# Two transformer blocks in fp32: gate and up products with high and low activations in one 512-column stretch, chunk products in halves

## The chip, the cores and the metric

The kernel runs on one core of a Trainium2 chip. The metric is the device time of one execution in microseconds; lower is better. A core has a matrix engine (TensorE, PE in the rows; its weight loads are PEld), a vector engine (VectorE, DVE), a scalar engine (ScalarE, ACT), GpSimd (POOL) and SyncE (SP), which here issues nearly all the weight transfers. Each engine works through its own list of instructions in order and waits on semaphores for the others. PE writes only to PSUM; ACT and DVE read it from there.

## What is computed

The reference is two blocks of layers, each of depth 2, on 256 tokens of width 1024, all in fp32. The change touches the first block alone:

```python
def first_block(x, p, positions, ...):
    h = x
    for i in range(DEPTH):                      # DEPTH = 2
        a = rms_norm(h, attn_norm[i])
        proj = a @ w_in[i]                      # split into the inputs of three mixers
        y_da  = diff_attention(...)
        y_ssd = ssd_mixer(...)                  # chunked scan, chunks of 128
        y_gla = gla_mixer(...)                  # gated linear attention, chunks of 64
        h = h + concat(y_da, y_ssd, y_gla) @ w_out[i]
        f = rms_norm(h, ffn_norm[i])
        h = h + (silu(f @ w_ffn_gate[i]) * (f @ w_ffn_up[i])) @ w_ffn_down[i]   # D_FF = 2816
        h = h + sigmoid(h @ ple_w_gate[i]) * (p[i] @ ple_w_proj[i])
    return h
```

In `ssd_mixer` the product within a chunk is `y_diag = einsum('bclsgr,bcsgrp->bclgrp', cb * decay, xdt)`: for each of 2 chunks and 8 heads a 128 x 128 map, lower triangular, times 128 x 64 values. The second block (a gated scan and a latent attention, modulated by `silu(c) @ ada_w + ada_b`) needs the modulation rows `c @ ada_w`; the kernel computes those in the layers of the first block, in three turns of PSUM called mod0, mod1 and mod2 in each layer.

## The kernel before

**Precision.** Large products are made from pairs. Weights and activations are split into a high part, rounded to float32r, and a low part, what is left. ACT writes the high part of a piece of weights (`split_high`, one ACTIVATE at L563), DVE subtracts and writes the low part (`split_low`, L570). A product is then a `triple` of matmuls: weights high by activations low, weights low by activations high, and high by high, all three added up in one stretch of PSUM. Small products (transposes, chunk products, modulation) are plain fp32 matmuls. In the profile a plain fp32 matmul shows as two records, a transpose as one. L2575 is the line of `mm`, L2578 that of `tr`.

**Weights.** They stream through a ring of four slots of 1 MB in a fixed order. SP issues the transfer of a piece when PE has ended the piece four places ahead of it (L2176, and L2208 for `ada_w`); ACT splits it, DVE splits it, PE uses it.

**PSUM in turns.** The half named `pg` is two buffers of 1024 columns, `pm` two more. `GEMM = Turns(pg, ...)` holds a list of turns by name; turn number k lies in buffer k modulo 2 and may begin when turn k - 2 is released by whoever read it. `M = Turns(pm, ...)` is the same for the small products. So the position of a name in these lists decides whom PE waits for.

**Around the chunk products.** In each layer, after the input projections and the scores of attention, PE runs in program order: state, pv and gla_att (`pm`), six transposes kendT (`pm`), modulation(1), the states gla_st0 (`pm`, from kendT as ACT copied it), the 16 chunk products ydiag into one turn of `pg`, the eight transposes mix0, gla_st1, modulation(2), yoff, and then the output projection `wo_products`. ACT meanwhile copies: pv with its squares (L2479, L2482), kendT (L2488), then `gates_silu` (a table load and a Silu over 2048 columns, L2420), `modulation_rows(1)` (L2350, which releases the turn mod1), the split of wo1, the copy of ydiag (L2479), and so on. DVE folds gla_st0 into running states (`gla_state`, L3237 and L3240; the second call releases gla_st0), splits wo1, makes the low part of mix0 (L3255), folds gla_st1, adds ydiag and yoff (L3276 to L3280) and norms the SSD output (up to L3249). PE waits for that norm before the transposes mix1. The list of `pg` turns there is z, mod0, gg, mod1, ydiag, mod2, wo_t0, wo_t1. The list of `pm` turns is gla_att, kendT, gla_st0, mix0, gla_st1, yoff: gla_st1 takes the buffer of gla_st0.

**Gate and up.** D_FF has 22 blocks of 128 columns. A piece `gu{j}_{k}` holds one block of gate weights and the same block of up weights. `columns_by_tokens` takes two pieces a turn: for each piece, for gate and up, for the 8 chunks of the contraction, a triple with 128 x 128 weights stationary and 256 tokens moving. Two pieces fill one turn of 1024 columns. ACT then takes Silu of the gate half (L2519), DVE multiplies by the up half (L3320), rounds (L3322), subtracts (L3324) and releases the turn. The down projection (`rows_to_width`) follows.

## Time and profile before

| | |
|---|---|
| median of 3 runs | 1776.08 us |
| lowest, highest | 1774.67, 1778.15 us |
| the profiled execution | 1776.09 us |
| its span, first to last instruction | 1774.0 us |
| mean granted TensorE clock | 0.996 of full speed |
| PE busy, weight loads busy | 96%, 84% of the span |
| DVE, ACT, POOL busy | 68%, 51%, 3% |
| gate and up products of layer 0, of layer 1 | from 219.28 to 344.26 us, from 640.82 to 765.8 us |
| output stage of the mixers of layer 0, of layer 1 | 146 to 182 us, 566 to 604 us |

The profile is one execution seen by the hardware profiler. Times in its rows are us from the first instruction. An instruction's own duration contains its pipeline, so matmuls in a stream overlap: what one costs is the distance from its start to the next start, and a run of n matmuls that lasts T with a last duration of d costs (T - d) / (n - 1) each. "idle before <-" says how long the engine stood still before a row and who released it.

### The profile page before, as it was taken

How to read it: one execution, taken by the hardware profiler on the slowest of the kernel's cores; microseconds unless marked ns; L12 is line 12 of the kernel's file. 1: busy time of each engine (PE TensorE's matmuls, PEld its weight loads, DVE VectorE, ACT ScalarE, POOL GpSimd, SP SyncE). 2: the span in 40 equal slices, each digit the busy share in tenths (PEclk: the TensorE clock that was granted, in tenths of full speed). 3: DMA queues.
4: the chain of work that ended last, by engine and by line, in shares of the span. 5: the costliest groups of instructions: out<-in, count | busy, mean ns of one | idle time of the engine just before them, and what ended most of it. 6: DMA issues, size and time to landing. Idle time of an engine off the chain costs nothing.

```text
span 1774.0 us, 34217 instructions
## 1 busy us (share of the span) xinstructions
PE 1709.9 (96%) x14302; PEld 1487.3 (84%) x14302; DVE 1207.2 (68%) x1673; ACT 902.5 (51%) x1112; POOL 44.5 (3%) x47
## 2 busy tenths in 40 slices
PE   6999999998999999999999999999999989999998
PEld 5877799987987789988988888888888867899896
DVE  5888755546678765545557768678677795577874
ACT  5564443335475443334554556455454553466772
POOL 2000000000000000000000000000000000000130
PEclk9999999998999999999999999999999999999999
DMA  8557568654457566655321322222212122352112
GB/s 202 186 190 298 154 169 200 190 190 149 145 169 265 208 166 191 190 190 166 99 88 61 93 72 73 77 68 85 73 61 85 60 96 96 113 176 62 48 63 104
DMA packets 255241, 238.20 MB, mean 134 GB/s; under 512 B 32800, under 2 KB 218192, under 8 KB 254832
## 3 DMA queue, kind: packets, MB, share of 16 engines
q1 hardware_dynamic: 253952, 233.21, 42.4%
q0 software_dynamic: 1136, 2.81, 0.6%
q8 instruction: 113, 1.85, 0.4%
q14 instruction: 40, 0.33, 0.1%
HBM read 234.94 MB, written 1.05 MB: 133 GB/s over the span
## 4 chain that ended last, share of the span: by engine, by line
PE 81%; DVE 7%; ACT 4%; DMA 3%; SPq 2%; DVEq 2%; issue 1%; ACTq 1%
PE pg L2575 34%; PE pg L1279 34%; PE pm L1279 7%; PE pm L2575 2%; PE pm L1282 2%; SPq L2198 2%; DMA ring<-in_ada_w 1%; DVE ring_r L570 1%; DMA ring<-in_hg_w_in 1%; PE pm L2578 1%; DVE ring_r L1734 1%; ACT ring_r L563 1%; DVEq L1770 1%; DVE ring L1768 1%; DMA ring<-in_w_in 0%
## 5 line engine op out<-in xcount | busy, mean ns | idle before, releaser
L570 DVE TENSOR_TENSOR ring_r<-ring,ring_r 128x2048 fp32r<-128x2048 f32 (+1 forms) x126 | 283.5, 2260 | 151.2 <-ACT ring_r L563 145.6
L2575 PE MATMUL pg<-ring_r,work_r 128*128 128x512 f32 (+1 forms) x1776 | 377.3, 372 | 5.5 <-DVEq L3047 2.9
L2575 PEld LDWEIGHTS pg<-ring_r,work_r 128*128 128x128 f32 x1776 | 306.1, 189 | 68.6 <-issue 8.4
L1279 PE MATMUL pg<-ring_r,work_r 128*128 128x512 f32 (+3 forms) x1280 | 355.6, 383 | 5.1 <-DVE work_r L1740 3.5
L2575 PE MATMUL pg<-work_r,ring_r 128*128 128x256 f32 x2688 | 318.7, 281 | 6.8 <-DVE ring_r L570 3.7
L2575 PEld LDWEIGHTS pg<-work_r,ring_r 128*128 128x128 f32 x2688 | 317.3, 188 | 8.2 <-DVE ring_r L570 4.5
L563 ACT ACTIVATE ring_r<-ring 128x2048 fp32r<-128x2048 f32 (+1 forms) x126 | 237.1, 1890 | 167.6 <-DMA ring<-in_w_ffn_up 67.7
L1279 PE MATMUL pg<-ring_r 128*128 128x512 f32 (+3 forms) x752 | 284.2, 378 | 2.5 <-DVEq L783 1.4
L1279 PEld LDWEIGHTS pg<-ring_r,work_r 128*128 128x128 f32 x1280 | 235.5, 188 | 50.6 <-DVEq L1735 4.2
L1279 PE MATMUL pg<-work_r,ring_r 128*128 128x512 f32 (+1 forms) x976 | 264.1, 360 | 0.0
L1279 PEld LDWEIGHTS pg<-work_r,ring_r 128*128 128x128 f32 x976 | 173.0, 189 | 26.9
L1279 PEld LDWEIGHTS pg<-ring_r 128*128 128x128 f32 x752 | 141.6, 188 | 26.5 <-DVEq L783 1.6
L775 ACT ACTIVATE ring_r<-ring 128x1024 fp32r<-128x1024 f32 x80 | 84.9, 1061 | 53.9 <-DMA ring<-in_hg_w_in 46.9
L782 DVE TENSOR_TENSOR ring_r<-ring,ring_r 128x1024 fp32r<-128x1024 f32 x80 | 98.0, 1225 | 17.0 <-ACTq L776 10.9
L1768 DVE TENSOR_TENSOR work<-work 128x1024 f32<-128x1024 f32 x56 | 66.1, 1222 | 23.3 <-PE pm L1279 21.9
L1768 DVE TENSOR_TENSOR ring<-ring,work 128x1024 f32<-128x1024 f32 x56 | 66.1, 1222 | 15.7 <-PE pm L1279 14.3
L1279 PE MATMUL pg<-work_r,work_r 128*128 128x256 f32 (+1 forms) x360 | 73.7, 322 | 0.6 <-DVEq L1735 0.6
L968 ACT COPY prm<-ring 128x1024 f32<-128x1024 f32 x28 | 31.9, 1138 | 72.1 <-DVEq L1770 44.6
L968 ACT COPY prm<-work 128x1024 f32<-128x1024 f32 x28 | 32.0, 1144 | 65.4 <-DVEq L1770 42.1
L1279 PEld LDWEIGHTS pg<-work_r,work_r 128*128 128x128 f32 x360 | 57.6, 190 | 5.9 <-DVEq L1735 0.9
L1279 PE MATMUL pm<-work 128*32 128x32 f32 (+1 forms) x928 | 59.5, 233 | 0.0
L1279 PEld LDWEIGHTS pm<-work 128*32 128x32 f32 (+1 forms) x928 | 56.3, 146 | 2.8 <-issue 0.8
(382 smaller groups left out, 1858.6 us busy)
## 6 DMA issues: line engine op xcount, KB each, us to landing
ring<-in_w_in SPq DMA_DIRECT2D x36, 1024.0 KB, 5.1
ring<-in_ada_w SPq DMA_DIRECT2D x24, 1024.0 KB, 7.1
ring<-in_hg_w_in SPq DMA_DIRECT2D x48, 512.0 KB, 3.7
ring<-in_w_ffn_gate SPq DMA_DIRECT2D x44, 512.0 KB, 3.9
ring<-in_w_ffn_up SPq DMA_DIRECT2D x44, 512.0 KB, 5.2
ring<-in_w_ffn_down SPq DMA_DIRECT2D x22, 1024.0 KB, 4.8
ring<-in_hg_w_in SPq DMA_DIRECT2D x64, 256.0 KB, 2.9
ring<-in_w_out SPq DMA_DIRECT2D x12, 1024.0 KB, 4.9
```

What stands on the lines that cost most here:

```text
L563: W.high_done(A.activation(hi, W.raw(i, name)[:, 0:hi.shape[1]], ACT.Copy))
L570: W.low_done(V.tensor_tensor(lo, W.raw(i, name)[:, 0:lo.shape[1]], W.hi(i, name).bitcast(f32), ALU.subtract))
L775: A.activation(HS.hi(name), HW.slot(name), ACT.Copy)
L782: V.tensor_tensor(HS.lo(name), HW.slot(name), HS.hi(name).bitcast(f32), ALU.subtract)
L968: A.copy(k_level.rearrange("p (n r m) -> p n r m", r=2, m=1 << lev), halves_of(b, KF, KB, lev))
L1279: return T.matmul(out_, lhsT, rhs, start=first, stop=last)
L1282: return T.transpose(out_, in_, ident)
L1734: V.tensor_tensor(MP.lo(name)[:, 0:n], MP.raw(name)[:, 0:n], MP.hi(name)[:, 0:n].bitcast(f32), ALU.subtract)
L1768: V.tensor_tensor(ap[:, :, :, r, :], ap[:, :, :, r, :], dec[:, :, :, 1 - r, 0].unsqueeze(3).to_broadcast([P, 2, 512 // m, m]), ALU.mult)
L1770: event.set(dve.drain())
L2198: sp.dma_start(dst, src).then_inc(loaded_prm, 16)
L2575: return T.matmul(out_, lhsT, rhs, start=first, stop=last)
```

## The change

1. **Gate and up.** A view `work_pairs` of the whole work tile in float32r lets one matmul read the high and the low activations of a chunk as two stretches of 256 columns, one behind the other (`later_pair`). With the high weights stationary it writes 512 columns: high by high in the first 256, high by low in the last 256. A second matmul of 256 columns adds low weights by high activations to the first half. So 2 matmuls stand in place of a triple's 3, with the same number of moved columns. Each of the 22 pieces is a turn of PSUM of its own (gate in one bank, up in the other).
2. **Behind it.** ACT copies the high-by-low halves out of PSUM, DVE adds the other halves and releases the turn, ACT takes Silu of the gate, and DVE multiplies, rounds and subtracts, now on 256 columns a piece; the latter three run one piece later.
3. **Chunk products.** ydiag becomes two turns, ydiag0 and ydiag1, one a chunk. Each 128 x 64 product becomes two with 64 weight columns each, whose results go to partitions 0 to 63 and 64 to 127.
4. **Order on PE.** modulation(1) moves ahead of the kendT transposes, and ydiag0 and ydiag1 move ahead of gla_st0.
5. Two events for qT and kT become one that counts to two. Nothing moves by it.

The core of the diff:

```diff
         GEMM = Turns(pg, sem("gemm_filled"), [sem("gemm_free0"), sem("gemm_free1")],
-                     ["daq", "dak", "xbc0", "xbc1", "gqk", "dav", "gv", "z", "mod0", "gg", "mod1", "ydiag", "mod2", "wo_t0", "wo_t1"]
-                     + [f"gu{j}" for j in range(FC // 2)] + ["dn_t0", "dn_t1"] + ple_pieces)
+                     ["daq", "dak", "xbc0", "xbc1", "gqk", "dav", "gv", "z", "mod0", "gg", "mod1", "ydiag0", "ydiag1", "mod2", "wo_t0", "wo_t1"]
+                     + gu_pieces + ["dn_t0", "dn_t1"] + ple_pieces)
...
+        def later_pair(c):
+            row = work_pairs[:]
+            return bass.AP(row.tensor, row.offset + start(aT) + c * S, [list(row.ap[0]), [start(low_f) - start(aT), 2], [1, S]])
...
                 gates_silu()
                 modulation_rows(1)
                 split_high(act, i, wo_pieces[1])
-                part_in("ydiag", xdt, None, GEMM)
+                for t in range(NT):
+                    GEMM.wait_filled(act, f"ydiag{t}", i)
+                    GEMM.release(A.copy(xdt[:, t * 512:(t + 1) * 512], GEMM.buf(f"ydiag{t}")[:, 0:512]), f"ydiag{t}")
+                e_part.set(act.drain())
...
+                def gate_up_part(j):
+                    name = gu_pieces[j]
+                    GEMM.wait_filled(act, name, i)
+                    if j > 1:
+                        e_gu.wait(act, i, j - 1)
+                    src = GEMM.buf(name).rearrange("p (f r n) -> p f r n", f=2, r=2)
+                    e_gate.set(A.copy(q3(gate_up[:, (j % 2) * 512:(j % 2) * 512 + 512], 2), src[:, :, 1, :]))
+
+                def gate_silu(j):
+                    gate = gate_up[:, (j % 2) * 512:(j % 2) * 512 + S]
+                    e_gsum.wait(act, i, j + 1)
+                    e_gate.set(A.activation(gate, gate, ACT.Silu))
+
                 for k in range(3, len(later_pieces)):
-                    j = (k - 3) // 2
-                    if k % 2 == 0 and j < FC // 2:
-                        GEMM.wait_filled(act, f"gu{j}", i)
-                        e_sgate.set(A.activation(sgate[:, (j % 2) * 512:(j % 2) * 512 + 512], GEMM.buf(f"gu{j}")[:, 0:512], ACT.Silu))
+                    j = k - 3
+                    if j < FC:
+                        gate_up_part(j)
+                    if 0 < j <= FC:
+                        gate_silu(j - 1)
...
+                def gate_and_up(name):
+                    wh, wl = weights(name, KC, 256)
+                    GEMM.wait_free(pe, name, i)
+                    order = [(f, c) for f in range(2) for c in range(KC)]
+                    if name == gu_pieces[0]:
+                        order = [(f, 2 * q + c) for q in range(4) for f in range(2) for c in range(2)]
+                    for f, c in order:
+                        if name == gu_pieces[0] and f == 0 and c % 2 == 0:
+                            e_aT.wait(pe, i, 4 + c // 2 + 1)
+                        both, cs = GEMM.buf(name)[:, f * 512:(f + 1) * 512], slice(f * P, (f + 1) * P)
+                        if c == 0:
+                            mm(both, wh[:, c, cs], later_pair(c), True, False)
+                            mm(both[:, 0:S], wl[:, c, cs], A_LATER[0][:, c, :], False, False)
+                        else:
+                            mm(both[:, 0:S], wl[:, c, cs], A_LATER[0][:, c, :], False, False)
+                            last = mm(both, wh[:, c, cs], later_pair(c), False, c == KC - 1)
+                    GEMM.done(last)
...
                 M.done(last)
+                modulation(1)
                 M.wait_free(pe, "kendT", i)
...
-                modulation(1)
...
+                e_mt.wait(pe, i)
+                for t in range(NT):
+                    GEMM.wait_free(pe, f"ydiag{t}", i)
+                    for hd in range(SSD_H):
+                        for q in (0, 64):
+                            at = t * 1024 + hd * P + q
+                            last = mm(GEMM.buf(f"ydiag{t}")[q:q + 64, hd * 64:(hd + 1) * 64], big[:, at:at + 64],
+                                          xdt[:, t * 512 + hd * 64:t * 512 + (hd + 1) * 64])
+                    GEMM.done(last)
                 e_kendT.wait(pe, i)
                 e_gv.wait(pe, i)
                 gla_states("gla_st0", (0, 1))
...
+                def gate_up_sum(j):
+                    name, both = gu_pieces[j], q3(gate_up[:, (j % 2) * 512:(j % 2) * 512 + 512], 2)
+                    e_gate.wait(dve, i, at_part(j))
+                    src = GEMM.buf(name).rearrange("p (f r n) -> p f r n", f=2, r=2)
+                    GEMM.release(V.tensor_tensor(both, both, src[:, :, 0, :], ALU.add), name)
+                    e_gsum.set(dve.drain())
```

On PE, at the chunk products of layer 0, the rows of before are these. The transposes in the first row are kendT, `ring,prm` is modulation(1), the first 128x256 is gla_st0, 128x64 is ydiag:

```order
L2578 MATMUL pm<-cst,work 128x128 [waits mixer_psum_free1]
L2578 MATMUL pm<-cst,work 128x128 x5
L2575 MATMUL pg<-ring,prm 32x256 [waits ada_weights_ready0,gemm_free0]
...
L2575 MATMUL pg<-ring,prm 32x256 x7
L2575 MATMUL pm<-work 128x256 [waits mixer_psum_free0,gv_in,kendT_in]
L2575 MATMUL pm<-work 128x256 x3
L2575 MATMUL pg<-work 128x64 [waits gemm_free1,ssd_maps]
L2575 MATMUL pg<-work 128x64 x15
L2578 MATMUL pm<-cst,work 128x128 [waits mixer_psum_free1,mixer_out]
```

The same place on PE after the change (64x64 are the halves of ydiag0 and ydiag1):

```order
L2602 MATMUL pg<-ring,prm 32x256 [waits ada_weights_ready0,gemm_free0]
...
L2602 MATMUL pg<-ring,prm 32x256 x7
L2605 MATMUL pm<-cst,work 128x128 [waits mixer_psum_free1]
L2605 MATMUL pm<-cst,work 128x128 x5
L2602 MATMUL pg<-work 64x64 [waits gemm_free1,ssd_maps]
L2602 MATMUL pg<-work 64x64 x15
L2602 MATMUL pg<-work 64x64 [waits gemm_free0]
L2602 MATMUL pg<-work 64x64 x15
L2602 MATMUL pm<-work 128x256 [waits mixer_psum_free0,gv_in,kendT_in]
L2602 MATMUL pm<-work 128x256 x3
L2605 MATMUL pm<-cst,work 128x128 [waits mixer_psum_free1,mixer_out]
```

modulation(1) now stands first, the chunk products stand ahead of gla_st0, and their second half has a wait of its own, on gemm_free0: the buffer that mod1 was in.

On ACT at the same place, after the change (L2497 copies kendT, L2429 is `gates_silu`, L2359 is `modulation_rows(1)`, L571 splits wo1, L2504 copies ydiag0 and ydiag1); before it the rows stood in this same order, with one copy of 1024 columns for ydiag:

```order
L2497 COPY work<-pm 128x768 [waits mixer_psum_filled]
L2429 ACT_TABLE_LOAD
L2429 ACTIVATE work<-work 128x2048
L2359 COPY work<-pg 128x256 [waits gemm_filled]
L571 ACTIVATE ring_r<-ring 128x2048 [waits gemm_filled,weights_ready2]
L2504 COPY work<-pg 128x512 [waits gemm_filled] x2
L2482 ACTIVATE work_r_12800<-pm,prm 128x1024 [waits mixer_psum_filled]
```

Only the copy of ydiag changed here: no row moved past another.

On PE in the middle of a gate or up block, before (work_r_22040 is the low part of the activations, work_r_4096 the high part):

```order
L2575 MATMUL pg<-work_r_4096,ring_r 128x256 x2
L2575 MATMUL pg<-work_r_22040,ring_r 128x256
L2575 MATMUL pg<-work_r_4096,ring_r 128x256 x2
L2575 MATMUL pg<-work_r_22040,ring_r 128x256
```

and after:

```order
L2602 MATMUL pg<-work_pairs,ring_r 128x256
L2602 MATMUL pg<-work_pairs,ring_r 128x512
L2602 MATMUL pg<-work_pairs,ring_r 128x256
L2602 MATMUL pg<-work_pairs,ring_r 128x512
```

Three matmuls of 256 columns became one of 256 and one of 512.

## Rows read from the trace of the kernel before

**Rows 1.** The page: the chain that ended last, share of the span by engine.

```profile
PE 81%; DVE 7%; ACT 4%; DMA 3%; SPq 2%; DVEq 2%; issue 1%; ACTq 1%
```

**Rows 2.** Timeline, PE, gate and up products of layer 0: start, duration, line, operation, count.

```profile
225.44 0.73 PE L2575 MATMUL pg<-work_r,ring_r 128*128 128x256 f32 x4 [0.28 <-DVE ring_r L570]
...
230.72 112.52 PE L2575 MATMUL pg<-work_r,ring_r 128*128 128x256 f32 x954
```

**Rows 3.** Timeline, PE: streams of 512-column matmuls, and a change from 256 to 512.

```profile
24.50 16.77 PE L2575 MATMUL pg<-ring_r,work_r 128*128 128x512 f32 x71 [0.23 <-DVE ring_r L570]
...
349.77 50.48 PE L2575 MATMUL pg<-ring_r,work_r 128*128 128x512 f32 x222
...
882.06 0.28 PE L1279 MATMUL pg<-work_r,ring_r 128*128 128x256 f32 x1
...
882.54 0.40 PE L1279 MATMUL pg<-ring_r 128*128 128x512 f32 x1
...
883.93 0.39 PE L1279 MATMUL pg<-ring_r 128*128 128x512 f32 x1
```

**Rows 4.** Groups by line and form, DVE and ACT, from 225.4 to 344.2 us.

```profile
L570 DVE TENSOR_TENSOR ring_r<-ring,ring_r 128x2048 fp32r<-128x2048 f32 x22 | 50.3, 2292 | 28.0 <-ACT ring_r L563 26.6
L563 ACT ACTIVATE ring_r<-ring 128x2048 fp32r<-128x2048 f32 x21 | 40.2, 1913 | 33.3 <-DMA ring<-in_w_ffn_up 30.6 <-DMA ring<-in_w_ffn_down 2.7
L3320 DVE TENSOR_TENSOR work<-work,pg 128x512 f32<-128x512 f32 x10 | 6.9, 688 | 18.9 <-ACT work L2519 18.9
L2519 ACT ACTIVATE work<-pg 128x512 f32<-128x512 f32 x10 | 6.0, 597 | 36.6 <-PE pg L2575 36.6
```

**Rows 5.** Timeline, PE, around the chunk products of layer 0.

```profile
145.90 5.13 PE L2575 MATMUL pm<-work 128*128 128x256 f32 x44 [0.37 <-ACT work L2462]
152.17 0.88 PE L2578 MATMUL pm<-cst,work 128*128 128x128 f32 x6 [1.13 <-ACT work L2482]
152.97 3.66 PE L2575 MATMUL pg<-ring,prm 128*32 128x256 f32 x64
156.56 1.99 PE L2575 MATMUL pm<-work 128*128 128x256 f32 x8
158.39 3.68 PE L2575 MATMUL pg<-work 128*128 128x64 f32 x32
161.91 1.04 PE L2578 MATMUL pm<-cst,work 128*128 128x128 f32 x8
162.79 1.03 PE L2575 MATMUL pm<-work 128*128 128x256 f32 x4
...
166.73 1.07 PE L2575 MATMUL pg<-ring,prm 128*32 128x256 f32 x16 [0.18 <-DMA ring<-in_ada_w]
...
168.51 3.79 PE L2575 MATMUL pg<-ring_r,work_r 128*128 128x512 f32 x15
```

**Rows 6.** Timeline, ACT, the same place.

```profile
153.08 0.80 ACT L2488 COPY work<-pm 128x768 f32<-128x768 f32 x1 [0.96 <-PE pm L2578]
...
157.27 0.37 ACT L2350 COPY work<-pg 128x256 f32<-128x256 f32 x1
```

**Rows 7.** Timeline, DVE, the same place: the two folds of gla_st0.

```profile
158.66 1.20 DVE L3237 COPY work<-pm 64x128 f32<-64x128 f32 x4
159.94 1.43 DVE L3240 SCALAR_TENSOR_TENSOR work<-work,pm 64x128 f32<-64x128 f32 x4
```

**Rows 8.** Timeline, PE: layer 1, the same place, and the next wait of layer 0.

```profile
179.01 1.09 PE L2578 MATMUL pm<-cst,work 128*128 128x128 f32 x8 [0.21 <-DVEq L3250]
...
588.24 1.07 PE L2575 MATMUL pg<-ring,prm 128*32 128x256 f32 x16 [1.61 <-DMA ring<-in_ada_w]
```

**Rows 9.** Timeline, SP, the issues of the `ada_w` pieces of modulation(2).

```profile
154.10 2.96 SPq L2208 DMA_DIRECT2D ring<-in_ada_w  x4
```

**Rows 10.** Stretches of the trace, PE alone: length, busy (x), granted clock, DMA share, GB/s.

```profile
441.00:443.00 2.00, 2.00 (x5) 0.50 0.00 0
```

**Rows 11.** Timeline, PE: the long wait between the layers.

```profile
436.28 3.68 PE L2578 MATMUL pm<-cst,work 128*128 128x128 f32 x16 [4.96 <-DVE work L3012]
```

## What the change should do to the time

> **What bounds the kernel now.** I read the chain that ended last first: 81% of the span is PE [rows 1], and PE is busy for 96% of it. So an instruction taken from PE's stream is worth its distance to the next start, and a new wait of PE is worth its length, unless something later waits anyway. Then I read PE's timeline in the two places that the change touches. In the gate and up products PE runs without a wait: after one of 0.28 us for the low weights of the second piece, 954 matmuls stand in one row [rows 2]. Around the chunk products PE's list is short pieces of work that alternate with copies on ACT and DVE, with waits of 1.13 us for ACT (L2482) and of 0.18 us for `ada_w` [rows 5]. The second of these is 1.61 us in layer 1 [rows 8]. There ACT and DVE must be read beside PE [rows 6, 7].
>
> **Gate and up: what a group of matmuls costs.** Before, 954 matmuls of 256 columns take 112.52 us, the last lasting 0.28: (112.52 - 0.28) / 953 = 0.1178 us each, 0.3533 a triple. After, a triple is one of 512 columns and one of 256. Moved columns are the same, so the gain can only be the fixed cost of one matmul. The trace has long streams of 512 at two rates [rows 3]: (50.48 - 0.39) / 221 = 0.2267, and (16.77 - 0.39) / 70 = 0.2340, which holds a small hesitation. It has no alternation of the two sizes. Right behind 256-column matmuls the 512s come every (883.93 - 882.54) / 6 = 0.2317 us (the shown rows are the first and the last of seven starts), and the 256s ahead of them every (882.54 - 882.06) / 4 = 0.120. In the new stream every 512 follows a 256, which is this case, and every 256 follows a 512.
>
> A low estimate of the pair is 0.2267 + 0.1178 = 0.3445, and one from the rows around the change of size is 0.2317 + 0.120 = 0.3517. I take the middle, 0.348. As ends I keep 0.2267 + 0.110 = 0.337 (0.110 is (161.91 - 158.39) / 32, the pace of matmuls with 128 weight columns and hardly any moved ones, [rows 5]) and 0.2340 + 0.120 = 0.354, which is no gain at all. That the moving operand is now in two stretches lies inside these ends; no row shows it, and the order of reads by rows of 256 is what the triples did.
>
> A piece has 16 triples, a layer 22 pieces. The first piece gains nothing: it is fed by DVE, and the second starts when DVE has split its weights, at 225.44, whatever PE did [rows 2]. So 21 x 16 = 336 groups a layer: 336 x (0.3533 - 0.348) = 1.8 us, **3.6 us in both layers**, with ends of 11 us and -0.5 us.
>
> The Trainium skill, page "TensorE: Matmul & The Clock Gate", section "Back-to-back issue gap", gives a warm gap of the columns over 2.4 GHz plus 2.5 ns. By it a triple would cost 327.5 ns and the new pair 325.0, an estimate of 0.8 us a layer and 1.7 in all in place of 3.6. The rows above show about 11 ns over the columns for a 256 and 13 to 18 for a 512, so the trace doesn't agree with its constant, and I go by the rows.
>
> **Gate and up: what moves to ACT and DVE.** A piece lasts 16 x 0.348 = 5.6 us on PE. In it ACT has a split (1.91 us), a copy of 512 columns out of PSUM (as L2519, 0.60) and a Silu of 256 (about 0.35, somewhat over half of 0.60): 2.9 us. DVE has a split (2.29), a sum of 512 (as L3320, 0.69) and three steps of 256 (the product at 512, L3320, takes 0.69; I take 1.1 for the three halves): 4.1 us [rows 4]. Both fit. The turn is released after a copy and a sum, about 1.4 us after PE filled it, and PE wants the buffer 5.6 us after: cost zero, and if ACT or DVE were held up PE would have 4 us before it noticed. Weights: piece k is split after piece k - 3 is done and used two pieces later, at least 11 us for about 5 us of splitting. Transfers are issued by PE's progress as before. Cost zero.
>
> **Chunk products and their order: PE step by step, layer 0.** The 1.13 us wait goes, since modulation(1) needs nothing that is late: its 64 records at 152.97 show no wait for `ada_w` [rows 5]; that they are there 2 us earlier is not shown, and I take it so, since the transfers were issued one behind the other as modulation(0) freed their slots, well before. It starts at 145.90 + 5.13 = 151.03 and takes 156.56 - 152.97 = 3.59: to 154.62. The kendT transposes take 0.80: to 155.42. Then ydiag0. A 64-weight product can't be paced by 0.110 any more; its 64 moved columns cost 64 x 0.229 / 256 = 0.057 (gla_st0: (158.39 - 156.56) / 8 = 0.229 for 256), and two halves write different partitions. The modulation matmuls, four strips of 32, take 3.59 / 64 = 0.056 each where a lone one of 256 columns takes 0.229: strips run side by side. So 64 records x 0.057 / 2 = 1.8 us in both turns (0.9 each) where 3.52 stood; side by side or not is open, and the end without it is 3.65. ydiag0 ends at 156.3.
>
> Now ydiag1 waits for the buffer of mod1, and what releases it is ACT's L2350. ACT's order has not changed: copy of kendT, table load and Silu of 2048 columns, then L2350. From the start of the kendT copy to the end of L2350 is 157.27 + 0.37 - 153.08 = 4.56 us [rows 6]. Before, kendT came early and mod1 ran beside the Silu. Now kendT is there at 155.5, so L2350 ends at 160.1. **PE waits 3.8 us** and does ydiag1 until 161.0. Behind the waiting matmul are gla_st0, mix0, gla_st1 and modulation(2). gla_st0 (1.83) ends at 162.9. DVE, which was at work on it from 158.66 to 161.37 [rows 7], starts at 163.0 and releases it after 2.71 us, at 165.7. PE does mix0 (0.88, to 163.7) and **waits 2.0 us** for that release before gla_st1. From gla_st1 to the output products took 168.51 - 162.79 = 5.72 us with 0.18 of waiting, so 5.54: they start at 171.3, **2.8 us late**.
>
> The wait for `ada_w` in modulation(2) goes: its four pieces are issued as modulation(1) frees their slots, from 154.10 before [rows 9], 1.9 us earlier now, and PE comes 3 us later. That is the 0.18 above, and in layer 1 it is 1.61. Layer 1 has the same schedule 420.08 us later ((588.24 - 1.61) - (166.73 - 0.18), the moments at which PE began to wait), so it loses 2.8 - (1.61 - 0.18) = 1.4 us. Is the loss taken back later? The next wait is for the norm of the SSD output, 0.21 us at 179.01 [rows 8]; its input is the copy of yoff, which is late by the same 2.8, so nothing is there to take it. **Sum: +4.2 us.** The ends are +3 (shorter transitions) and +6 (halves not side by side: 0.9 us more a layer before DVE can start).
>
> **The sum.** +4.2 - 3.6 = +0.6 us. The profiled execution took 1776.09 us, the median of three is 1776.08, so the forecast is 1776.7 us. A measurement of this kernel can tell about 0.2%, or 3.6 us, from no change. The forecast is inside.
>
> **Rivals.**
>
> *The pairs run faster.* If weight loads are all that holds a 256 behind a 512, the group costs under 0.342 and the gain is over 7.6 us. At 0.340 it is 672 x 0.0133 = 8.9, and the time is 1776.1 + 4.2 - 8.9 = 1771.4. For it: one matmul in three is gone and the fixed cost is some 11 ns. Against it: 512s behind 256s are slower in the rows, 0.2317. Chance 0.17.
>
> *PE doesn't wait at ydiag1.* If L2350 came in time, ydiag would end at 157.3, gla_st0 at 159.1, DVE at 161.8, and the output products would start some 1.2 us early in layer 0 and 2.6 in layer 1: 1776.1 - 3.8 - 3.6 = 1768.7. The order and the durations on ACT speak against it. Chance 0.06.
>
> *The clock falls in the new wait.* After a wait of 4.96 us [rows 11] PE is granted 0.50, its 1.2 GHz level, and still has it from 441 to 443 us [rows 10]; what it did before was to stand idle. The new wait of 3.8 us is shorter, but longer than the 1.61 us before the last part of modulation(2) in layer 1; over the whole span the mean grant is 0.996, so the short waits cost no clock. If the clock falls, ydiag1 and gla_st0 (2.7 us) take twice as long, and gla_st1 likewise: 3.5 us a layer. In both layers: 1776.7 + 7 = 1783.7; in one, 1780.2. It is decided by whether the idle time of 3.8 us is enough. Chance 0.14.
>
> *Slow pairs and chunk halves that run one after the other.* Pairs at 0.354 (+0.5) and 0.9 us a layer: 1776.1 + 4.2 + 0.5 + 1.8 = 1782.6. Chance 0.06.
>
> **How the numbers follow.** The forecast has 0.57, all of it within 0.2%. Faster is the first two rivals, 0.23; slower the last two, 0.20; same 0.57. The range reaches to the first rival below, 1771, and above to the clock falling in one layer with some of the open cost, 1781.5; that leaves out about 0.2.
>
> **What would show it.** The group: the count and length of PE's stream in the gate and up products, 0.348 x 16 = 5.57 us a piece where it was 5.65; 704 matmuls a layer for 1056. The wait: a row of 64-column weights with some 3.8 us idle before it, ended by ACT's copy of mod1, and one of 2 us before gla_st1, ended by DVE; the wait for `ada_w` gone in both layers; the output products 2.8 us later after the start of pv in layer 0. The clock: 1.00 in these stretches. I am wrong if ydiag1 starts without a wait, if the group costs less than 0.342 or more than 0.354, or if PE waits anywhere inside the gate and up products.

## The result, and the profile after

The changed kernel takes 1781.94 us (median of 20 executions, 1777.91 to 1784.1) beside 1776.38 for the kernel before on the same chip (20 executions, 1774.49 to 1779.57). The ratio is 1.0027, with a 95% interval of 1.0021 to 1.0033: **slower by 4.8 us**, and by 5.6 in the medians. The forecast was 1776.7 and no change, with a range from 1771 to 1781.5. The profiled execution took 1783.84 us, with a span of 1781.7 and a mean granted clock of 0.992.

Timeline of PE, around the chunk products of layer 0, to be read beside [rows 5]:

```profile
147.36 5.13 PE L2602 MATMUL pm<-work 128*128 128x256 f32 x44 [0.38 <-ACT work L2471]
152.42 3.66 PE L2602 MATMUL pg<-ring,prm 128*32 128x256 f32 x64
156.01 0.87 PE L2605 MATMUL pm<-cst,work 128*128 128x128 f32 x6
156.81 1.15 PE L2602 MATMUL pg<-work 128*64 128x64 f32 x32
161.54 1.98 PE L2602 MATMUL pg<-work 128*64 128x64 f32 x32 [3.57 <-ACT work L2359]
163.45 3.78 PE L2602 MATMUL pm<-work 128*128 128x256 f32 x8
167.02 1.23 PE L2605 MATMUL pm<-cst,work 128*128 128x128 f32 x8
170.10 1.41 PE L2602 MATMUL pm<-work 128*128 128x256 f32 x4 [1.85 <-DVE work L3281]
171.44 5.01 PE L2602 MATMUL pg<-ring,prm 128*32 128x256 f32 x64
176.38 1.13 PE L2602 MATMUL pm<-work 128*128 128x256 f32 x4
177.16 1.05 PE L2602 MATMUL pg<-ring_r,work_r 128*128 128x512 f32 x3
```

The order is the one foreseen: the 1.13 us ahead of the kendT transposes is gone, PE stands 3.57 us before ydiag1 until ACT has copied mod1 (L2359), and then stands 1.85 us before gla_st1 for DVE, and modulation(2) is one row without a wait for `ada_w`. But two durations don't fit. The second turn of 32 half products lasts 1.98 us where the first lasts 1.15, and gla_st0 lasts 3.78 us for 8 matmuls that took 1.99 before [rows 5]. modulation(2) lasts 5.01 where modulation(1), the same 64 matmuls, lasts 3.66. The stretches of the same trace tell why (length, then PE, PEld, DVE, ACT, POOL busy, granted clock, DMA share, GB/s):

```profile
158.00:160.00 2.00, 0.00 (x0) 0.00 (x0) 1.85 (x2) 1.99 (x2) 0.00 (x0) 1.00 1.01 418
160.00:162.00 2.00, 0.46 (x8) 0.46 (x10) 0.00 (x0) 1.74 (x3) 0.00 (x0) 0.64 1.02 420
162.00:164.00 2.00, 2.00 (x31) 1.83 (x28) 0.00 (x0) 2.00 (x3) 0.00 (x0) 0.50 1.03 418
164.00:166.00 2.00, 2.00 (x6) 1.60 (x5) 0.00 (x0) 0.52 (x2) 0.00 (x0) 0.50 0.74 295
166.00:168.00 2.00, 2.00 (x11) 1.62 (x10) 0.64 (x3) 0.00 (x0) 0.00 (x0) 0.65 0.01 2
168.00:170.00 2.00, 0.25 (x3) 0.01 (x1) 1.86 (x6) 1.11 (x1) 0.00 (x0) 1.00 0.00 0
170.00:172.00 2.00, 1.90 (x12) 1.01 (x16) 1.91 (x2) 0.00 (x0) 0.00 (x0) 0.70 0.04 8
172.00:174.00 2.00, 2.00 (x24) 0.86 (x20) 1.83 (x3) 0.00 (x0) 0.00 (x0) 0.50 0.00 0
```

PE does nothing from 158 to 160, and before its wait is over the granted clock begins to fall (0.64 from 160 to 162) to 0.50, the 1.2 GHz level. It falls a second time behind the wait of 1.85 us. In the kernel before it is 1.00 in every such stretch here, in both layers. In layer 1 of after it falls twice as well: gla_st0 lasts 3.55 us and modulation(2) 4.97. There the 32 half products right behind the wait still last 1.15 us, at the full clock, and the fall comes only with gla_st0 behind them.

The Trainium skill, page "TensorE: Matmul & The Clock Gate", Part 1, section "What's actually happening", says of this clock that "the default state is throttled, and activity releases the throttle". The trace agrees as far as it goes: the clock falls in a wait or shortly behind one, and is back at 1.00 from 168 us on, when PE has worked through gla_st0, until the next wait.

From the start of pv (147.36) to the first output product (177.16) is 29.80 us in layer 0 and 28.75 in layer 1. Before it was 22.61 (168.51 - 145.90, [rows 5]) and 24.04. That is +7.2 and +4.7, where the forecast had +2.8 and +1.4. Behind it nothing is caught up and nothing more is lost in layer 0: from the first output product to the first gate and up product is 50.77 us in both kernels.

The two profiled executions also differ where nothing was changed, so the medians are a better measure than these two. After comes to pv in layer 0 1.46 us later (147.36 against 145.90), and to pv in layer 1 5.73 us later, where 1.46 + 7.2 - 1.1 = 7.6 would be due: between the layers, behind the wait of [rows 11], its clock was at 0.50 for a shorter time. And it has one more fall, behind a wait of 1.89 us in the input projections of layer 0 (a row of PE's timeline, then a stretch as above):

```profile
70.40 13.38 PE L2602 MATMUL pg<-work_r,ring_r 128*128 128x256 f32 x96 [1.89 <-DVE ring_r L578]
...
72.00:74.00 2.00, 2.00 (x11) 2.00 (x11) 1.92 (x5) 0.94 (x2) 0.00 (x0) 0.50 0.37 140
```

This one cost nothing: from the start of that row to the next is 13.22 us here, and 13.20 in another execution of the same program (e10 below), where the clock stays at 1.00 and PE waits 1.53 us for DVE halfway instead.

Timeline of PE, gate and up products of layer 0, beside [rows 2]:

```profile
227.93 5.80 PE L2602 MATMUL pg<-work_pairs,ring_r 128*128 128x512 f32 x32 [1.54 <-DVEq L3078]
234.10 117.84 PE L2602 MATMUL pg<-work_pairs,ring_r 128*128 128x512 f32 x672 [0.37 <-DVE ring_r L578]
351.78 8.59 PE L2602 MATMUL pg<-ring_r,work_r 128*128 128x512 f32 x37
```

21 pieces of 16 pairs take 351.78 - 234.10 = 117.68 us, so a pair is 0.3502 by this row, where a triple was 0.3533: by its instructions, a matmul behind a 256 starts after 117.0 ns, one behind a 512 after 233 (229 to 239). The stage is 123.85 us long (before: 124.98), so it is 1.13 us a layer shorter, 2.3 in all, where the forecast had 3.6. The pairs make 336 x 3.1 ns = 1.04 of the 1.13; the other 0.1 is not placed.

ACT and DVE behind it, groups by line and form in that stretch (count, then busy us, mean ns, idle before), beside [rows 4]:

```profile
L3358 DVE TENSOR_TENSOR work<-work,pg 128x512 f32<-128x512 f32 x21 | 14.5, 689 | 20.3 <-ACT work L2534 20.3
L2534 ACT COPY work<-pg 128x512 f32<-128x512 f32 x21 | 12.3, 587 | 57.3 <-PE pg L2602 57.3
L3369 DVE TENSOR_TENSOR work_r<-work,work_r 128x256 fp32r<-128x256 f32 x20 | 8.5, 426 | 1.6
L3365 DVE TENSOR_TENSOR work<-work 128x256 f32<-128x256 f32 x20 | 8.5, 425 | 2.7
L2539 ACT ACTIVATE work<-work 128x256 f32<-128x256 f32 x20 | 8.4, 421 | 0.0
L3367 DVE CAST work_r<-work 128x256 fp32r<-128x256 f32 x20 | 5.9, 293 | 1.6
```

DVE's four steps of a piece sum to 0.689 + 0.425 + 0.293 + 0.426 = 1.83 us, ACT's two to 1.01; with the splits that is 4.1 and 2.9 of 5.6 us, as forecast, and PE waits nowhere inside but the 0.37 us at the second piece (0.28 before).

### The profile page after: what moved, and what is told of

Same layout as the page of the kernel before. It is cut to its first block, busy times and chain, and to the rows that moved or that the text cites. A ratio compares the mean times of both kernels' runs of the same rounds, so it can differ in the third digit from the quotient of the medians.

```text
span 1781.7 us, 33287 instructions
## 1 busy us (share of the span) xinstructions
PE 1712.6 (96%) x13662; PEld 1455.1 (82%) x13662; DVE 1246.3 (70%) x1783; ACT 926.4 (52%) x1180; POOL 44.4 (2%) x47
## 4 chain that ended last, share of the span: by engine, by line
PE 81%; DVE 7%; ACT 4%; SPq 2%; DVEq 2%; DMA 1%; issue 1%; ACTq 1%
PE pg L1288 34%; PE pg L2602 34%; PE pm L1288 8%; PE pm L2602 3%; PE pm L1291 2%; SPq L2207 2%; DVE ring_r L578 1%; PE pm L2605 1%; DMA ring<-in_w_in 1%; ACT ring_r L571 1%; DVEq L1779 1%; DVE ring L1777 1%; DVE ring_r L1743 1%; DMA ring<-in_hg_w_in 0%; SPq L2185 0%
## 5 line engine op out<-in xcount | busy, mean ns | idle before, releaser
L571 ACT ACTIVATE ring_r<-ring 128x2048 fp32r<-128x2048 f32 (+1 forms) x126 | 237.2, 1888 | 108.3 <-DMA ring<-in_w_ffn_down 53.3
L2602 PE MATMUL pg<-work_pairs,ring_r 128*128 128x512 f32 (+1 forms) x1408 | 247.3, 337 | 3.8 <-DVEq L3078 3.1
L2602 PEld LDWEIGHTS pg<-work_pairs,ring_r 128*128 128x128 f32 x1408 | 215.1, 188 | 35.9 <-issue 3.5
L1288 PEld LDWEIGHTS pg<-work_r,ring_r 128*128 128x128 f32 x976 | 173.0, 189 | 27.3
L2534 ACT COPY work<-pg 128x512 f32<-128x512 f32 x44 | 25.8, 587 | 122.1 <-PE pg L2602 122.1
L2602 PE MATMUL pg<-work_r,ring_r 128*128 128x256 f32 x576 | 71.0, 285 | 2.3 <-DVE ring_r L578 2.3
L2602 PEld LDWEIGHTS pg<-work_r,ring_r 128*128 128x128 f32 x576 | 70.0, 192 | 3.3 <-DVE ring_r L578 3.1
```

The lines of the kernel that those rows point to most:

```text
L571: W.high_done(A.activation(hi, W.raw(i, name)[:, 0:hi.shape[1]], ACT.Copy))
L1288: return T.matmul(out_, lhsT, rhs, start=first, stop=last)
L2534: e_gate.set(A.copy(q3(gate_up[:, (j % 2) * 512:(j % 2) * 512 + 512], 2), src[:, :, 1, :]))
L2602: return T.matmul(out_, lhsT, rhs, start=first, stop=last)
```

## The experiments

All times are medians; "ratio" is to the kernel before on the same chip, with its 95% interval. The last column is the time from the start of pv to the first output product in layers 0 and 1 of the profiled execution, with * where the granted clock fell in it. The kernels did not all run on one chip: the kernel before took 1777.35 us beside e1 to e4, 1776.23 beside e5 to e8 and 1776.86 beside e9 to e12. So a difference of medians between two of these groups is good to about 1 us, and the ratios are given beside it.

| kernel | us | ratio | pv to output products |
|---|---|---|---|
| before | 1776.38 | | 22.61, 24.04 |
| after | 1781.94 | 1.0027 [1.0021, 1.0033] | 29.80*, 28.75* |
| e1_fill | 1779.82 | 1.0013 [1.0005, 1.0022] | 27.19*, 25.56 |
| e2_rows_first | 1771.6 | 0.9966 [0.9954, 0.9978] | 23.40*, 22.03 |
| e3_mod_back | 1774.35 | 0.9982 [0.9973, 0.999] | 23.18, 24.87* |
| e4_gu_only | 1775.83 | 0.9984 [0.9976, 0.9993] | 22.57, 23.90 |
| e5_best | 1769.56 | 0.996 [0.9945, 0.9975] | 21.18, 21.69 |
| e6_triples | 1772.83 | 0.9983 [0.9974, 0.9993] | 23.40*, 21.96 |
| e7_grouped | 1770.26 | 0.9966 [0.9954, 0.9977] | 23.40*, 22.09 |
| e8_full | 1774.45 | 0.999 [0.9981, 0.9998] | 23.13, 24.76* |
| e9_two_fills | 1779.29 | 1.0011 [1.0002, 1.002] | 25.57, 25.56 |
| e10_after_again | 1782.06 | 1.0025 [1.0014, 1.0037] | 27.11*, 25.55 |
| e11_rows_again | 1771.48 | 0.9961 [0.9949, 0.9974] | 23.46*, 21.96 |
| e12_best_again | 1770.59 | 0.9964 [0.9951, 0.9978] | 20.84, 21.95 |

The theory was: the new wait before ydiag1 costs its length, and the granted clock that falls in it or behind it costs the rest. The rival: the two orders and the pairs have costs of their own that the profile shows only in part, and the clock is chance.

**e1_fill: the wait filled with idle products.** The edit against after; the products go to the half of ydiag0's buffer that nobody reads:

```diff
                 for t in range(NT):
+                    if t:
+                        for _ in range(4):
+                            mm(GEMM.buf("ydiag0")[:, 512:1024], ones, cst[:, 0:512])
                     GEMM.wait_free(pe, f"ydiag{t}", i)
```

> The changed kernel with four fp32 matmuls of constants, 512 columns each, put on PE between ydiag0 and ydiag1 (into the unused bank of ydiag0's buffer, read by nobody). They last about 3.5 us, as long as the wait for the buffer of mod1, and lengthen nothing. Theory: the wait lets the granted clock fall to 0.50, which costs 4.4 us in layer 0 and 3.3 us in layer 1 of the profiled run beside the waits themselves. Then with the engine kept at work the clock stays at 1.00, ydiag1 to gla_st0 take 2.7 us, and the time is about 1776.4 + 4.2 - 2.2 = 1778.4 us. Rival: the slow ydiag1, gla_st0 and modulation(2) come from something else (the half-width form, the order): then the time stays at 1782 us and the stretch stays slow.

Measured: 1779.82. In its profile gla_st0 lasts 1.99 us again, in both layers. In layer 0 the clock still falls, behind the other wait:

```profile
162.29 1.15 PE L2602 MATMUL pg<-work 128*64 128x64 f32 x32
163.37 1.99 PE L2602 MATMUL pm<-work 128*128 128x256 f32 x8
165.21 1.04 PE L2605 MATMUL pm<-cst,work 128*128 128x128 f32 x8
168.24 1.46 PE L2602 MATMUL pm<-work 128*128 128x256 f32 x4 [2.00 <-DVE work L3284]
169.63 4.96 PE L2602 MATMUL pg<-ring,prm 128*32 128x256 f32 x64
```

So the first fall is gone in both layers and the second is not in layer 0. The median is 1.4 us over the expectation, which had not thought of that second place; the fall there cost 27.19 - 25.56 = 1.6 us in this profile.

**e9_two_fills and e10_after_again: both waits filled, and the changed kernel beside it.** Two such products more, ahead of gla_st1:

```diff
                 mixed_transposes(0)
+                for _ in range(2):
+                    mm(GEMM.buf("ydiag1")[:, 512:1024], ones, cst[:, 0:512])
                 gla_states("gla_st1", (2,))
```

> The changed kernel with four idle products of 512 columns of ones between the two turns of chunk products (as e1_fill) and two more ahead of the second GLA state products, where TensorE otherwise waits 2.00 us for VectorE. No operation of another engine moves. Theory (the granted clock falls in waits): the modulation products behind that wait take 3.66 us in both layers and no stretch of that part shows less than 1.00; e1_fill had 4.96 us in its first layer and 1.00 in its second. 1778.6 us, some 1.2 us under e1_fill's 1779.82, and 3.3 us under the changed kernel. Rival (the clock falls for the traffic of the chip or at random, whatever TensorE does there): as e1_fill, 1779.8 us, and falls in the profile as before.

> The changed kernel itself beside e9_two_fills, on the same chip. All theories: 1782 us, and a wait of 3.57 us ahead of the second turn of chunk products in both layers, with a granted clock under 1.00 behind it both times.

Measured: 1779.29 against 1782.06 on the same chip, 2.8 us less in the medians with six products more a layer. The intervals of these two ratios overlap, 1.0002 to 1.002 and 1.0014 to 1.0037; that of after's 20 executions, 1.0021 to 1.0033, and e9's do not. e9 shows 1.00 in every stretch of this part in both layers, and its two layers take the same time, 25.57 and 25.56. By its ratio, though, it isn't told from e1 (1.0011 and 1.0013), so what the second fill is worth alone stays open. Nor do the two profiled executions show the gain: e9's took 1779.91 us, 1.5 more than e10's, mostly because the fall between the layers lasted longer in it (last section). The gain stands on the medians.

e10 is the same program as after and tells more. Its profiled execution took 1778.38, 5.5 us less than that of after. The waits are nearly the same (2.00 us before gla_st1 where it was 1.85 and 1.87), but in this part the clock fell once where it fell four times. Timeline of PE, e10, layer 0 and then layer 1:

```profile
157.60 1.15 PE L2602 MATMUL pg<-work 128*64 128x64 f32 x32
162.33 1.97 PE L2602 MATMUL pg<-work 128*64 128x64 f32 x32 [3.57 <-ACT work L2359]
164.23 2.72 PE L2602 MATMUL pm<-work 128*128 128x256 f32 x8
...
583.92 1.15 PE L2602 MATMUL pg<-work 128*64 128x64 f32 x32 [3.58 <-ACT work L2359]
585.00 1.99 PE L2602 MATMUL pm<-work 128*128 128x256 f32 x8
```

And its stretches:

```profile
162.00:164.00 2.00, 1.67 (x32) 1.67 (x32) 0.00 (x0) 1.83 (x2) 0.00 (x0) 0.58 1.01 408
164.00:166.00 2.00, 2.00 (x11) 1.59 (x9) 0.00 (x0) 1.31 (x3) 0.00 (x0) 0.57 1.03 424
...
584.00:586.00 2.00, 2.00 (x37) 1.83 (x38) 0.00 (x0) 1.69 (x1) 0.00 (x0) 1.00 1.03 416
```

I had expected falls in both layers: a miss. The same wait of 3.57 us is followed by a fall in one layer and not in the other. All 27 executions of this program show what the clock does to the time: the 17 with a mean granted clock of 0.991 to 0.994 took 1780.57 to 1784.1 us (median 1782.6), the 10 with 0.995 to 0.997 took 1777.91 to 1782.91 (median 1778.8). Their mean clock is 0.9939, that of e9's executions 0.9963.

**e2_rows_first, and again as e11: what PE waits for comes first on ACT.** The edit against after, on ACT:

```diff
                 part_in("pv", mix3[:, :, 0:512], sc)
+                modulation_rows(1)
                 M.wait_filled(act, "kendT", i)
...
                 gates_silu()
-                modulation_rows(1)
```

> The changed kernel with one line of ACT moved: modulation_rows(1), which releases the buffer that ydiag1 takes, stands ahead of the kendT copy and gates_silu. Theory (the wait at ydiag1 is ACT's order alone): PE goes from kendT through ydiag0, ydiag1 and gla_st0 without a wait, waits about 1.9 us for DVE before gla_st1, the clock stays at 1.00, and the output products start 1.2 us earlier than in the kernel before in layer 0 and 2.6 us in layer 1. With 2.2 us from gate and up that is 1776.4 - 3.8 - 2.2 = 1770.4 us. Rival (the order of PE costs by itself, since DVE starts on gla_st0 late): 1776 us or more.

> e2_rows_first itself, beside e12_best_again on the same chip. 1771.6 us; the wait of 2.00 us ahead of the second GLA state products stands in both layers, and the granted clock behind it falls in none, one or two of them (one in e2_rows_first's profile, the first layer; one in e3_mod_back's, the second).

Measured: 1771.6 and 1771.48, faster than before by 0.34% and 0.39%, and 10.3 us under after in the medians (10.8 by the ratios). Timeline of PE, layer 0 of e2:

```profile
157.30 2.09 PE L2602 MATMUL pg<-work 128*64 128x64 f32 x64
159.31 1.99 PE L2602 MATMUL pm<-work 128*128 128x256 f32 x8
161.14 1.04 PE L2605 MATMUL pm<-cst,work 128*128 128x128 f32 x8
164.18 1.68 PE L2602 MATMUL pm<-work 128*128 128x256 f32 x4 [2.00 <-DVE work L3281]
165.79 4.74 PE L2602 MATMUL pg<-ring,prm 128*32 128x256 f32 x64
```

The 64 half products stand in one row: the wait before ydiag1 is gone, so it was ACT's order alone that made it, and the rival (1776 us or more) is out. The expectation was 1.2 us too low and wrong about the clock: in this profile it falls behind the wait of 2.00 us in layer 0, which comes to 23.40 us. The layer without a fall is 25.56 - 22.03 = 3.5 us shorter than a layer with after's order and no fall (e9, e10), the length of the wait. In both layers that is 7.1. That the falls that went with the wait make up most of the other 3.2 is an inference from what is left over, close to the 2.8 between e9 and e10; it was not measured by itself.

**e3_mod_back: only modulation(1) back in its old place** (behind the kendT transposes, with ACT's order as in after):

```diff
                 M.done(last)
-                modulation(1)
                 M.wait_free(pe, "kendT", i)
...
                         last = tr(M.buf("kendT")[:, c * 256 + f * P:c * 256 + (f + 1) * P], src[:, f * S + t * P:f * S + (t + 1) * P])
                 M.done(last)
+                modulation(1)
```

> The changed kernel with modulation(1) back behind the kendT transposes, as before the change; chunk products in halves, in two turns, ahead of gla_st0. Theory: kendT is early again, so ACT's copy, Silu and modulation_rows(1) run beside modulation(1), ydiag1 waits 0.3 us at most, no clock is lost, DVE gets gla_st0 2 us later than before the change, and modulation(2) ends when its ada_w pieces land, as before: the chunk part costs about nothing against the kernel before, and the time is 1776.4 - 2.2 = 1774.2 us. Rival (the early chunk products or the halves are what costs): 1778 us or more.

Measured: 1774.35, as expected in the time. In its profile the clock fell once, in layer 1 behind the wait of 2.00 us before gla_st1 (24.87*), which the expectation did not have. So it is the move of modulation(1), not that of ydiag ahead of gla_st0 nor the halves, that makes after slow: with it alone undone the kernel is 7.6 us faster. Done together with the one line on ACT it is worth 2.8 us (e2 against e3), of which the traces have 1.14 a layer: e3 waits so long for ACT (L2491) before the kendT transposes, and e2 doesn't.

**e4_gu_only: the gate and up part alone,** with the full-width chunk products and the order of before, though still in two turns.

```diff
-                for t in range(NT):
-                    GEMM.wait_free(pe, f"ydiag{t}", i)
...
                 gla_states("gla_st0", (0, 1))
+                for t in range(NT):
+                    GEMM.wait_free(pe, f"ydiag{t}", i)
+                    for hd in range(SSD_H):
+                        last = mm(GEMM.buf(f"ydiag{t}")[:, hd * 64:(hd + 1) * 64], big[:, t * 1024 + hd * P:t * 1024 + (hd + 1) * P],
...
```

> The gate and up part of the change alone: PE's order around the chunk products as in the kernel before, products 128 wide, only that their two chunks lie in two turns of PSUM. Theory: the gate and up products gain 1.1 us a layer (0.3517 us a pair against 0.3533 a triple), nothing else differs: 1776.4 - 2.2 = 1774.2 us. Rival (the gate and up part costs something outside its own stretch): 1776 us or more.

Measured: 1775.83, ratio 0.9984, which is -2.8 us with an interval of -4.3 to -1.2; the medians differ by 1.5 on this chip. The trace's 2.3 lies in the interval. The rival (1776 us or more) is hardly apart from the median; against it speaks the trace, whose chunk part lasts 22.57 and 23.90 us, as in before. Timeline of PE in its gate and up products:

```profile
227.97 117.86 PE L2602 MATMUL pg<-work_pairs,ring_r 128*128 128x512 f32 x672 [0.35 <-DVE ring_r L578]
```

**e6_triples and e7_grouped: what a pair costs.** Both against e2. e6 takes the pairs apart again but keeps pieces, turns and the work of ACT and DVE:

```diff
-                        if c == 0:
...
+                        mm(both[:, S:2 * S], wh[:, c, cs], A_LATER[1][:, c, :], c == 0, False)
+                        mm(both[:, 0:S], wl[:, c, cs], A_LATER[0][:, c, :], False, False)
+                        last = mm(both[:, 0:S], wh[:, c, cs], A_LATER[0][:, c, :], False, c == KC - 1)
```

> e2_rows_first with the 512-column products taken apart again: three products of 256 columns for each block, as before the change, but with the pieces, PSUM turns and the work of ScalarE and VectorE of the change. If the stage goes at TensorE's pace alone, a block takes 0.3533 us again instead of 0.3517 and the kernel is 336 blocks x 2 layers x 1.6 ns = 1.1 us slower than e2_rows_first's 1771.6: 1772.7 us. If the change's gain in that stage (1.13 us a layer) came from the turns and from later or earlier work of the other engines, it stays at 1771.6 us; then the pair is worth nothing.

e7 puts the 512s of a block behind each other instead of between 256s, in every piece but the first:

```diff
+                        mm(both, wh[:, 0, cs], later_pair(0), True, False)
+                        for c in range(KC):
+                            mm(both[:, 0:S], wl[:, c, cs], A_LATER[0][:, c, :], False, False)
+                        for c in range(1, KC):
+                            last = mm(both, wh[:, c, cs], later_pair(c), False, c == KC - 1)
...
```

> e2_rows_first with the order of the products inside a block of 128 outputs changed: one of 512 columns, eight of 256 with the low weights, then seven of 512, instead of 512 and 256 in turn. Theory A (a 512-column product costs 229 to 239 ns only because the one before it is short, and would take 227 ns behind another long one): a block of eight takes some 30 ns less, 0.348 us a pair, and the kernel comes to 1771.6 - 2.2 = 1769.4 us. Theory B (the mean of a pair is set by columns and weight loads whatever the order): 1771.6 us. Rival C (eight short ones in a row, each with a new weight load, go at 118 ns as before the change): 1771.6 to 1772.2 us.

e6: 1772.83, which is 1.2 us over e2 in the medians and 3.0 by the ratios; e7: 1770.26, within the scatter of e2 and e11. Their streams (timeline of PE, layer 0), e6:

```profile
227.32 118.99 PE L2602 MATMUL pg<-work_pairs,ring_r 128*128 128x256 f32 x1008 [0.27 <-DVE ring_r L578]
```

and e7:

```profile
226.84 118.02 PE L2602 MATMUL pg<-work_pairs,ring_r 128*128 128x512 f32 x672 [0.35 <-DVE ring_r L578]
```

With everything else equal, 1008 short matmuls are a row of 118.99 us, and 672 in pairs one of 117.84 to 118.02. So the gain is PE's pace, 1.1 us a layer; the times of whole executions, whose scatter is as large, only don't contradict it. (The expectation had 1.1 for both layers: it took the pair at 0.3517, the mean of the stage with the waits in it, against a triple without them. Without waits it is 0.3502, and 2.3 us in all, which lies between the medians' difference and that of the ratios.) In e7 a matmul behind a 512 starts after 232 ns in the mean (225 to 238), one behind a 256 after 119, together 0.351; that is no better. Theory A falls: the 512s are not slowed by the short ones ahead of them. Why they go at 232 here and at 227 in the down projection of [rows 3] stays open.

**e8_full: the halves undone** (e2 with eight products of 128 rows a turn):

```diff
-                        for q in (0, 64):
-                            at = t * 1024 + hd * P + q
-                            last = mm(GEMM.buf(f"ydiag{t}")[q:q + 64, hd * 64:(hd + 1) * 64], big[:, at:at + 64],
+                        last = mm(GEMM.buf(f"ydiag{t}")[:, hd * 64:(hd + 1) * 64], big[:, t * 1024 + hd * P:t * 1024 + (hd + 1) * P],
...
```

> e2_rows_first with the chunk products of the first step as eight of 128 rows in each of the two turns instead of sixteen of 64. By the before kernel's row (32 products in 3.52 us against 64 in 2.09 to 2.29 us for two halves that run side by side) the halves are worth 1.3 us a layer where TensorE is the one waited for: 1771.6 + 2 x 1.3 = 1774.2 us. Rival (VectorE is waited for behind them, so the time is swallowed by the wait of 2.00 us ahead of the second GLA state products): between 1771.6 and 1772 us.

Measured: 1774.45, 2.9 us over e2 in the medians (2.6 expected), 4.3 by the ratios. PE's row of 32 is 3.68 us long where 64 halves take 2.09, and the wait for DVE behind them is 2.00 in both: it moves along, because DVE starts on the fold (L3276 here, L3278 in e2) when gla_st0 is done:

```profile
156.56 3.68 PE L2602 MATMUL pg<-work 128*128 128x64 f32 x32
...
162.13 1.20 DVE L3276 COPY work<-pm 64x128 f32<-64x128 f32 x4 [2.32 <-PE pm L2602]
```

**e5_best, and again as e12: gla_st0 between the two turns.** From that last reading, against e2:

```diff
-                for t in range(NT):
+                for t in (0,):
...
                 gla_states("gla_st0", (0, 1))
+                for t in (1,):
+                    GEMM.wait_free(pe, f"ydiag{t}", i)
...
```

> The changed kernel with ScalarE's modulation rows ahead of its copy of the chunk's keys (as in e2_rows_first), and on TensorE the first GLA state products between the two turns of chunk products, as the kernel before had them behind the chunk products. VectorE gets the GLA state 1 us earlier, so the wait of 2.00 us ahead of the second GLA state products should shrink to about 1 us in both layers. Theory (TensorE's waits and its granted clock there set the end): 1769.5 us if 1 us a layer comes off 1771.6, and 1766 us if the granted clock then also stays at 1.00 through the modulation products behind that wait (4.74 us back to 3.66 us). Rival (VectorE is the bound there, and TensorE's order is worth nothing): 1771.6 us.

> e5_best itself, beside e11_rows_again on the same chip. Theory (TensorE is waited for there, and the 0.77 us wait lets the clock stand): 1769.6 us, 2.0 us under e11_rows_again, and a granted clock of 1.00 in both layers. Rival (the two differed by chip and by chance): within 0.7 us of e11_rows_again.

Timeline of PE, layer 0 of e5:

```profile
155.78 1.15 PE L2602 MATMUL pg<-work 128*64 128x64 f32 x32
156.87 1.99 PE L2602 MATMUL pm<-work 128*128 128x256 f32 x8
158.79 1.15 PE L2602 MATMUL pg<-work 128*64 128x64 f32 x32
159.87 1.09 PE L2605 MATMUL pm<-cst,work 128*128 128x128 f32 x8
161.73 1.13 PE L2602 MATMUL pm<-work 128*128 128x256 f32 x4 [0.77 <-DVE work L3289]
162.79 4.01 PE L2602 MATMUL pg<-ring,prm 128*32 128x256 f32 x64
```

The wait for DVE is 0.77 us in all four layers seen, and the clock is 1.00 throughout. Measured: 1769.56 and 1770.59. So the 1766 us that e5's expectation gave for the case that the clock stays did not come though it stayed: e2 has a fall in one of its two layers and not in both, worth 23.40 - 22.03 = 1.4 us, so there was that much to win back and no more, and part of it went into waits for `ada_w`. Ten executions of this program have a median of 1769.7 (1767.71 to 1774.29), ten of e2's 1771.5 (1767.95 to 1772.43). On the shared chip the difference was 0.9 us, between what the theory (2.0) and the rival (under 0.7) gave, and the ratios to before are 0.9961 for e11 and 0.9964 for e12, with intervals that overlap. That it beats the kernel before, by 0.36 to 0.4%, is sure; that it beats e2 is likely by the medians and not shown by the ratios. Those waits for `ada_w` are of 0.14 and 0.58 us in modulation(2) of e5, and of 0.83 in layer 1 of e12.

## Where the prediction was right and where it was wrong, point by point

The forecast of no change was wrong: the kernel is slower by 0.27%, clear of the scatter. The median of 1781.94 lies 0.4 us over the range; put on the forecast's own base, 1776.1 x 1.0027 = 1780.9 lies in it, since the range reached up for a fall of the clock. Two terms of the sum failed, the pair and the clock, and both to the same side.

- **PE's order and its waits: right.** Forecast 3.8 us before ydiag1, ended by the copy of mod1, and 2.0 before gla_st1; measured 3.57 and 1.85 to 2.00. The two halves run side by side (2.0 us for both turns in e2, 1.8 forecast). The wait for `ada_w` is gone. In layers without a fall of the clock (layer 0 of e9, whose idle products fill the waits and move nothing else, and layer 1 of e9 and e10) the output products are 25.57 - 22.61 = 3.0 us late in layer 0 and 25.56 - 24.04 = 1.5 in layer 1: **+4.5** where the sum had +4.2. Nothing behind took it back, as said.
- **The work that moves to ACT and DVE, and the first piece: right,** at zero.
- **The pair: mis-sized.** The step that failed is "I take the middle, 0.348". Measured is 0.3502, nearer to the 0.3517 of the rows around a change of size [rows 3] than to the 0.3445 that joined the paces of two uniform streams: the 256 costs 0.117, as in a uniform stream, but the 512 costs 0.233 and not 0.2267, and e7 shows that even a run of 512s in this stage costs 0.232. The gain is 2.3 us, not 3.6. The Trainium skill, page "TensorE: Matmul & The Clock Gate", section "Back-to-back issue gap", would have given 1.7 with its 2.5 ns over the columns, which it states for a matmul by itself. In this stream each matmul has a weight load: 117.0 ns for a 256 is 10 over the columns, and 229 to 239 for a 512 is 16 to 26 over, so the trace doesn't agree with the constant, though 1.7 lies nearer to the 2.3 measured than 3.6 does.
- **The clock: the term left out of the sum.** It stood as a rival with 0.14 and 1780.2 to 1783.7; 1781.94 lies between. The order and the pairs alone give 4.5 - 2.3 = +2.2 us, and e9, with both waits filled, is 2.4 over before on its chip. The remaining 2.8 us between the medians of e10 and e9 came with the clock: the mean grants of their executions are 0.9946 and 0.9963. What failed is the argument from the mean grant: "over the whole span the mean grant is 0.996, so the short waits cost no clock" speaks of waits up to 1.6 us (most of the missing 0.004 is the fall at the one of 4.96), and the new ones are longer. Behind the wait of 2.0 us before gla_st1 the rival counted gla_st1 alone; the falls there reach into modulation(2), which lasts 5.01 us in place of 3.66. A fall costs less than the rival's 3.5 us a layer when it comes alone (27.11 - 25.57 = 1.5 in e10, 1.6 in e1), and about as much when both waits bring one (29.80 - 25.57 = 4.2 and 28.75 - 25.56 = 3.2). It doesn't come in every execution, so the median lies between the cases.
- **Together:** forecast +0.6; +0.3 from the order, +1.3 from the pair, +2.8 from the clock make +5.0, and 5.2 (e10) to 5.6 (after) were measured in the medians, 4.4 to 4.8 by the ratios. The rest is inside the scatter.

## What to carry to other kernels

When a producer is moved up on one engine, move up its consumer on the other one too: modulation(1) ahead of kendT cost 7.6 us as long as ACT kept its order (e3 against after), and brought 2.8 once one call on ACT moved with it (e2 against e3). Price a new wait of a PE that is otherwise busy at its length and, from the 1.85 us on that were followed by a fall here, add the matmuls behind it at half clock with a chance below one. Look at what PE waits for next, too: a fall whose lost time ends in a wait that comes anyway is free, as the one at 72 us is in after. For mixed sizes of matmuls take the pace nearer to the rows where the sizes change than to the fastest uniform stream.

## What the runs showed of the hardware

- **A wait of 1.9 to 2.0 us is enough for the clock, sometimes.** Eight profiles (e1, e2, e3, e6, e7, e8, e10, e11) have a wait of 2.00 us ahead of gla_st1 in each layer: 16 waits with a clock of 1.00 before them, and 7 of them are followed by 0.50. Behind the waits of 3.57 us it was 3 of 4. Behind the waits of 1.85 and 1.87 us before gla_st1 in after it was both times, shortly behind another fall. Behind those of 1.86 to 1.89 us for DVE's low weights at about 70 us, which all 13 kernels but the one before have, it was 2 (after, e2) of 13. Behind those of 0.77 (e5, e12) and 0.28 us (e9) before gla_st1 it was none of 6, nor did any of the many waits of 1.1 to 1.6 us in the 14 profiles bring one. What decides within one length stays open; the same program fell in one layer and not in the other.
- **How long a fall lasts differs as well.** The wait between the layers [rows 11] brings one in each of these profiles. In stretches of 2 us the granted clock is under 1.00 there from 442 to 448 us in after, from 442 to 446 in e10, and from 438 to 450 in e9, with the same work on PE. The transposes and the 96 matmuls of 512 columns behind the wait take 3.68 and 24.64 us in e9, 3.48 and 22.56 in e10. That alone is 2.3 us between two executions, and it is why a single profile can't price a change of 2 us here.
- **Idle products can pay.** e9 does six matmuls of 512 columns more a layer in PE's waits, and was 2.8 us faster in the medians than the same kernel without them. Taking the wait before ydiag1 away (e2) was worth nearly four times as much, 10.3.
